# Products of the two first mixers' inputs: pairs of tiles as 2x2 block products with seven multiplications

## The reference, cut to what matters

```python
def even_mixer(x, w_in, w_out):
    h = x @ w_in                                      # 512x1024 times 1024x3584
    rq, rk, rv, rg, sq, sk, sv = jnp.split(h, EVEN_SPLITS, axis=-1)
    ...                                               # rotary on rq, rk; silu on rg; attention
def odd_mixer(x, w_in, w_out, ...):
    h = x @ w_in                                      # 512x1024 times 1024x3072
    q, k, v = jnp.split(h, 3, axis=-1)
```

## Time and profile before

| | us |
|---|---|
| median of 3 runs (lowest, highest) | 2689.16 (2664.75, 2702.93) |
| profiled execution, first to last instruction (its whole time isn't given) | 2679.4 |
| TensorE busy | 2603.0 |
| VectorE, ScalarE, GpSimd busy | 1483.2, 1241.3, 114.9 |
| even_in, first to last matmul | 13.59 to 175.95 |
| odd_in, full tiles | 730.97 to 839.78 |

### The profile page before, as it was taken

The page is one execution under the profiler, slowest core; times in us unless marked ns, Lnnn a source line. Parts: engine busy times, 40 slices in busy tenths (PEclk is TensorE's granted clock), DMA queues, the critical chain, the costliest instruction groups (busy, mean ns, idle before and its releaser), DMA issues.

```text
span 2679.4 us, 51068 instructions
## 1 busy us (share of the span) xinstructions
PE 2603.0 (97%) x20904; PEld 2408.2 (90%) x20904; DVE 1483.2 (55%) x2490; ACT 1241.3 (46%) x2037; POOL 114.9 (4%) x178
## 2 busy tenths in 40 slices
PE   8999999999999999999999999989999999999998
PEld 8985999999997599999989877779966998999998
DVE  5235666543424776664467989862476354544433
ACT  4237344432425844442364887852475243444422
POOL 0000000000000000000001223300000000000000
PEclk9999999999998999999999999999999999999999
DMA  6420122223321023233344665632211231323232
GB/s 198 122 71 1 64 95 94 94 96 106 113 95 63 9 72 102 96 99 118 101 159 147 212 196 186 189 126 97 93 55 56 95 126 41 102 94 97 99 103 71
DMA packets 76142, 278.34 MB, mean 104 GB/s; under 512 B 9802, under 2 KB 12010, under 8 KB 75488
## 3 DMA queue, kind: packets, MB, share of 16 engines
q1 hardware_dynamic: 62112, 217.42, 24.3%
q0 software_dynamic: 13888, 58.88, 7.6%
HBM read 267.03 MB, written 9.24 MB: 103 GB/s over the span
## 4 chain that ended last, share of the span: by engine, by line
PE 77%; DVE 12%; ACT 6%; DMA 3%; issue 2%; POOL 0%; DVEq 0%; SPq 0%; ACTq 0%
PE acc L348 64%; PE acc L379 3%; DMA w_raw<-in_stream 2%; DVE big L1851 1%; PE ps L379 1%; DVE res_tmp L2150 1%; DVE big L2479 1%; ACT res_tmp L2120 1%; DVE w_lo L329 1%; PE acc L1351 1%; DVE big L1503 1%; ACT w_hi L323 1%; DVE res_tmp L2144 1%; PE ps L463 1%; PE ps L769 1%
## 5 line engine op out<-in xcount | busy, mean ns | idle before, releaser
L348 PE MATMUL acc<-x_split,w_hi 128*128 128x256 f32 x7936 | 1242.4, 279 | 7.7 <-ACT big L661 2.9
L348 PEld LDWEIGHTS acc<-x_split,w_hi 128*128 128x128 f32 x7936 | 1061.5, 189 | 10.6 <-issue 7.2
L348 PE MATMUL acc<-x_split,w_lo 128*128 128x256 f32 x3968 | 780.7, 278 | 0.0
L329 DVE TENSOR_TENSOR w_lo<-w_raw,w_hi 128x1024 fp32r<-128x1024 f32 x405 | 494.5, 1222 | 482.1 <-ACT w_hi L323 482.1
L323 ACT ACTIVATE w_hi<-w_raw 128x1024 fp32r<-128x1024 f32 x405 | 427.0, 1055 | 588.5 <-PE acc L348 525.7
L348 PEld LDWEIGHTS acc<-x_split,w_lo 128*128 128x128 f32 x3968 | 602.1, 189 | 0.0
L348 PE MATMUL acc<-big_r,w_hi 128*128 128x256 f32 x3376 | 528.4, 279 | 0.6 <-DVE big_r L2532 0.6
L348 PEld LDWEIGHTS acc<-big_r,w_hi 128*128 128x128 f32 x3376 | 451.7, 189 | 1.5 <-DVE big_r L2532 0.8
L348 PE MATMUL acc<-big_r,w_lo 128*128 128x256 f32 x1688 | 332.8, 279 | 0.0
L348 PEld LDWEIGHTS acc<-big_r,w_lo 128*128 128x128 f32 x1688 | 256.2, 188 | 0.0
L1066 ACT ACTIVATE res_tmp<-acc,par 128x512 f32<-128x512 f32 x84 | 64.8, 772 | 142.5 <-PE acc L348 138.0
(11 more groups left out here) (356 smaller groups left out, 2739.9 us busy)
## 6 DMA issues: line engine op xcount, KB each, us to landing
w_raw<-in_stream SPq DMA_DIRECT2D x405, 512.0 KB, 3.5
res_tmp<-scratch_rows POOLq DMA_DIRECT2D x96, 320.0 KB, 5.2
big<-scratch_rows POOLq DMA_DIRECT2D x32, 320.0 KB, 6.1
scratch_bias<-res_tmp POOLq DMA_DIRECT2D x1, 2560.0 KB, 56.0
res_tmp<-in_x SPq DMA_DIRECT2D x2, 1024.0 KB, 6.8
res_tmp<-scratch_bias POOLq DMA_DIRECT2D x8, 256.0 KB, 4.0
scratch_x<-res_tmp POOLq DMA_DIRECT2D x1, 2048.0 KB, 7.8
scratch_kv<-big POOLq DMA_DIRECT2D x1, 2048.0 KB, 8.3
```

What stands on the lines that cost most here:

```text
L329: dve.tensor_tensor(w_lo[:, u.slot], w_raw[:, u.slot], w_hi[:, u.slot].bitcast(F32), ALU.subtract).then_inc(lo_done, 1)
L348: mm = pe.matmul(a[:, h], w, AR[:, x + k, h], start=(k == 0 and w is wh and x == hi and h.start == 0), stop=(k == total - 1 and w is wl), ...
```

## The change

From tile 9 on (tiles 8 to 27 of even_in, 8 to 23 of odd_in, counted from 0) two tiles are computed as a pair, by Strassen's scheme in its form with few additions. Weights and inputs of a pair are 2x2 blocks: two output tiles by two halves of the 1024 inputs, and two halves of the inputs by two halves of the tokens. Seven block products (form f = 0 to 6) of 4 input blocks, 3 splits and 256 tokens, 12 matmuls each, are accumulated in three half banks a, b and c.

- `strassen_pool`: GpSimd makes four weight sums a pair (f = 1 to 4), each 128x512, in `w_sum`, which lies in the place of `w_lo`. Sum 2 is made from sum 1, sum 3 from sum 2; sum 1 needs both units of the pair.
- `st_hi` (ScalarE) rounds a form, `st_lo` (VectorE) writes its remainder over the sum; remainders 1 and 2 wait until sum 2 and sum 3 have read the sum in that place. The rings are now taken as eight half places: form n goes into place n mod 8, free once the product 8 forms before is done. A raw unit is given back with both of a pair, behind remainder 6.
- `strassen_act`: ScalarE copies three partial sums out of PSUM (snapshots 0 to 2, after products 0 to 2) and the last output quarter; each copy stands behind the rounding of the same form of the next pair. `strassen_dve`: VectorE adds the other three output quarters (additions 0 to 2, after products 3 to 5) between the remainders of the next pair. Product f = 2 to 4 waits for snapshot f - 2, product 6 for additions 0 and 1.
- `t_step`, `t_hi`, `t_lo`: in the first 8 tiles four sums of input blocks are made and split (eight sums and four remainders of 1024 columns on VectorE, four roundings on ScalarE).
- Thirteen semaphores get shared names (`SHARED`), to make room. The stages' matmuls on TensorE are written out instead of looped.

The diff, cut to its core:

```diff
+ST_FIRST, ST_PAIRS = 8, {"even_in": 10, "odd_in": 8}
+        ST_IN = ((XH, XL, 0, 0), (0, None), (1, None), (XH, XL, 4, 1), (2, None), (XH, XL, 4, 0), (3, None))
...
+        def st_place_free(eng, stage, n):
+            if n < 8:
+                tile_done(eng, Units(UB[stage] + ST_FIRST - RING + n // 2))
+            else:
+                st_multiplied(eng, stage, n - 8)
...
+        def strassen_pe(pe, stage):
+            for p in range(ST_PAIRS[stage]):
+                g, u, t = ST_BASE[stage] + p, st_unit(stage, p), st_tile(stage, p)
+                a, b, c = st_banks(t)
+                pe.wait_ge(acc_free[t.bank], t.in_bank + 1)
+                for f, to in enumerate((a, b, a, b, a, c, a)):
+                    if f == 6:
+                        pe.wait_ge(lo_done, u.count + 2)
+                        pe.wait_ge(ev("st_add"), 3 * g + 2)
+                    else:
+                        pe.wait_ge(ev("st_lo"), 6 * g + f + 1)
+                    if 2 <= f <= 4:
+                        pe.wait_ge(ev("st_snap"), 3 * g + f - 1)
+                    if p and f in (1, 5):
+                        pe.wait_ge(ev("st_add"), 3 * g - (2 if f == 1 else 0))
+                    if p == 0 and len(ST_IN[f]) == 2:
+                        pe.wait_ge(ev("t_lo"), 4 * (stage == "odd_in") + ST_IN[f][0] + 1)
+                    wh, wl = st_form(w_hi, 7 * p + f), st_form(w_lo, 7 * p + f)
+                    for k in range(4):
+                        cols = slice(k * P, k * P + P)
+                        for n, (w, lo) in enumerate(((wh, 0), (wh, 1), (wl, 0))):
+                            mm = pe.matmul(to, w[:, cols], st_x(stage, f, lo, k), start=(f in (0, 1, 5) and k == n == 0),
+                                           stop=(k == 3 and n == 2 and f in (3, 5, 6)), skip_group_check=True)
+                    if f == 6:
+                        mm.then_inc(units_used, 2)
+                    else:
+                        mm.then_inc(ev("st_used"), 1)
+        def st_hi(act, stage, p, f):
+            n, g = 7 * p + f, ST_BASE[stage] + p
+            st_place_free(act, stage, n)
+            if f in (0, 5, 6):
+                st_landed(act, stage, p, f // 6)
+                x = st_raw(stage, p, f // 6, f // 5)
+            else:
+                act.wait_ge(ev("st_sum"), 4 * g + f)
+                x = st_form(w_sum, n)
+            ins = act.activation(st_form(w_hi, n), x, ACT.Copy)
+            if f == 6:
+                ins.then_inc(hi_done, 2)
+            else:
+                ins.then_inc(ev("st_hi"), 1)
+        def st_sum(pool, stage, p, f):
+            n, g = 7 * p + f, ST_BASE[stage] + p
+            st_place_free(pool, stage, n)
+            if f == 1:
+                st_landed(pool, stage, p, 0)
+                st_landed(pool, stage, p, 1)
+                x, y, op = st_raw(stage, p, 1, 0), st_raw(stage, p, 1, 1), ALU.add
+            elif f == 2:
+                pool.wait_ge(ev("st_sum"), 4 * g + 1)
+                x, y, op = st_form(w_sum, n - 1), st_raw(stage, p, 0, 0), ALU.subtract
+            elif f == 3:
+                pool.wait_ge(ev("st_sum"), 4 * g + 2)
+                x, y, op = st_raw(stage, p, 0, 1), st_form(w_sum, n - 1), ALU.subtract
+            else:
+                x, y, op = st_raw(stage, p, 0, 0), st_raw(stage, p, 1, 0), ALU.subtract
+            pool.tensor_tensor(st_form(w_sum, n), x, y, op).then_inc(ev("st_sum"), 1)
+        def st_lo(dve, stage, p, f):
+            n, g = 7 * p + f, ST_BASE[stage] + p
+            if f == 6:
+                dve.wait_ge(hi_done, st_unit(stage, p).count + 2)
+                dve.wait_ge(ev("st_sum"), 4 * g + 4)
+            else:
+                dve.wait_ge(ev("st_hi"), 6 * g + f + 1)
+            if f in (1, 2):
+                dve.wait_ge(ev("st_sum"), 4 * g + f + 1)
+            x = st_raw(stage, p, f // 6, f // 5) if f in (0, 5, 6) else st_form(w_sum, n)
+            ins = dve.tensor_tensor(st_form(w_lo, n), x, st_form(w_hi, n).bitcast(F32), ALU.subtract)
+            if f == 6:
+                ins.then_inc(lo_done, 2)
+            else:
+                ins.then_inc(ev("st_lo"), 1)
+        def strassen_act(act, stage, out, scale=None, finish=None):
+            pairs = ST_PAIRS[stage]
+            for p in range(pairs):
+                g, u, t = ST_BASE[stage] + p, st_unit(stage, p), st_tile(stage, p)
+                a, b, c = st_banks(t)
+                by = scale(p) if scale else 1.0
+                after = 0
+                for f in range(7):
+                    if p + 1 < pairs:
+                        st_hi(act, stage, p + 1, f)
+                    if f < 3:
+                        act.wait_ge(ev("st_used"), 6 * g + f + 1)
+                        if f == 0 and p >= 2:
+                            act.wait_ge(ev("st_add"), 3 * (g - 2) + 3)
+                        act.activation(st_snap(stage, p, f), (a, b, a)[f], ACT.Copy, scale=by).then_inc(ev("st_snap"), 1)
+                    if f == 6:
+                        tile_done(act, u, 2)
+                        act.activation(out(p, 1, 0), a, ACT.Silu if finish and p in (2, 3) else ACT.Copy,
+                                       scale=by).then_inc(acc_free[t.bank], 1)
+                    while p + 1 == pairs and after < RING and st_last_form(stage, after) <= 7 * p + f:
+                        st_multiplied(act, stage, st_last_form(stage, after))
+                        split_hi(act, st_unit(stage, pairs) + after)
+                        after += 1
+                if finish:
+                    finish(p)
+        def strassen_dve(dve, stage, out, scale=None):
+            pairs = ST_PAIRS[stage]
+            for p in range(pairs):
+                g, t = ST_BASE[stage] + p, st_tile(stage, p)
+                a, b, c = st_banks(t)
+                by = scale(p) if scale else 1.0
+                after = 0
+                def add(n):
+                    dve.wait_ge(ev("st_used"), 6 * g + 4 + n)
+                    dve.wait_ge(ev("st_snap"), 3 * g + 3 - (n == 1))
+                    to, x = out(p, n == 1, n < 2), (b, a, c)[n]
+                    snap = st_snap(stage, p, (2, 1, 0)[n])
+                    if by == 1.0:
+                        ins = dve.tensor_tensor(to, x, snap, ALU.add)
+                    else:
+                        ins = dve.scalar_tensor_tensor(to, x, by, snap, ALU.mult, ALU.add)
+                    ins.then_inc(ev("st_add"), 1)
+                if p + 1 < pairs:
+                    q = p + 1
+                    st_lo(dve, stage, q, 0)
+                    st_lo(dve, stage, q, 1)
+                    st_lo(dve, stage, q, 2)
+                    add(0)
+                    st_lo(dve, stage, q, 3)
+                    add(1)
+                    st_lo(dve, stage, q, 4)
+                    st_lo(dve, stage, q, 5)
+                    add(2)
+                    st_lo(dve, stage, q, 6)
+                else:
+                    for n in range(3):
+                        add(n)
+                        split_lo(dve, st_unit(stage, pairs) + n)
+                    split_lo(dve, st_unit(stage, pairs) + 3)
+        def strassen_pool(pool, stage):
+            for p in range(ST_PAIRS[stage]):
+                for f in (1, 2, 3, 4):
+                    st_sum(pool, stage, p, f)
...
-                    split_hi(act, u + RING)
+                    if i == 0:
+                        split_hi(act, u + RING)
+                        continue
+                    for f in (2 * j, 2 * j + 1)[:2 - j // 3]:
+                        st_hi(act, "even_in", 0, f)
+                    t_hi(act, "even_in", j)
...
-                split_lo(dve, u + RING)
+                if n < 4:
+                    split_lo(dve, u + RING)
+                    for m in (2 * n, 2 * n + 1):
+                        t_step(dve, "even_in", m)
+                if n == 4:
+                    st_lo(dve, "even_in", 0, 0)
+                if n == 5:
+                    t_lo(dve, "even_in", 0)
+                    st_lo(dve, "even_in", 0, 1)
+                if n == 6:
+                    t_lo(dve, "even_in", 1)
+                    st_lo(dve, "even_in", 0, 2)
+                    st_lo(dve, "even_in", 0, 3)
+                if n == 7:
+                    t_lo(dve, "even_in", 2)
+                    for f in (4, 5, 6):
+                        st_lo(dve, "even_in", 0, f)
+                    t_lo(dve, "even_in", 3)
...
             pool.dma_start(SCR_BIAS, row).then_inc(ev("bias_out"), 16)
+            strassen_pool(pool, "even_in")
             pool.wait_ge(ev("bias_out"), 16)
...
                 pool.dma_start(A[:, DBIAS + h], row).then_inc(ev("bias_in"), 16)
+            strassen_pool(pool, "odd_in")
             pool.wait_ge(ev("g_lo"), 2 * KF)
```

More of the change, by code:

```diff
@@ L58 @@
 HEAD = {"up0": 0, "odd_in": 1, "up1": 2}
+ST_FIRST, ST_PAIRS = 8, {"even_in": 10, "odd_in": 8}
+ST_BASE = {"even_in": 0, "odd_in": 10}
 UB, TB = {}, {}
@@ new lines, in build, with st_unit, st_tile, st_form @@
```

(43 more changed lines are left out.)

162 lines of the change are left out of this document (121 added, 41 removed).

## The result

The median went from 2689.49 us (8 runs, 2662.74 to 2702.93) to **2708.52 us** (8 runs, 2686.69 to 2719.75); the ratio is 1.0077, with an interval of 1.0048 to 1.0107. The forecast was 2702 in a range of 2673 to 2724.

What follows compares the result with a forecast made beforehand. TensorE was taken to bound the kernel (busy 2603.0 of 2679.4 us), with late weight loads in even_in. Even_in +16, odd_in -3.9 and the seam +1 gave +13 on the median: 2702 us, range 2673 to 2724.

Steps and rivals of the forecast that it cites:

- (a): Matmuls in even_in and odd_in: 84 instead of 96 a pair, 9.52 us instead of 10.88, 24.5 us less in all.
- (b): Work beside each pair: sums and remainders wait for each other, last product 1.0 us late, pair 10.5; odd_in -3.9 us.
- the 11 that the forecast had named as a sign of being wrong: Changed profile: pairs 9.5 us apart or over 11 would show the prediction wrong; odd_in pairs about 10.5 apart, right.
- The two rows in which VectorE lost GpSimd's whole length: Later stage, VectorE additions beside GpSimd's: 1.55 us became 3.00, 1.28 became 2.38; a sum's hold was taken as 1.2.
- the row from 1738.40: Later stage: VectorE started 0.27 us before GpSimd yet lost the whole length, cited against the first issuer going first.
- (c): Preparing inputs in the first 8 tiles: in even_in VectorE at 5.5 us against 5.44, a lag under a microsecond.
- (d): Loads in even_in: units 12 and 13 asked for at 67 to 68, landing late; stage ends at 191.9, 16 us later.
- the gap: Weights' queue in even_in: after a gap the next load pays 22.9 us again; rival, nothing anew: 2692 us, chance 0.20.
- the table load: In even_in, 1.28 us ahead of a snapshot, with two gate activations: 1 us towards the stage's end.
- (e): End of even_in: two splits instead of one after the last product, 1 us on the path to the next stage.
- without a hold-up: Rival: sums and remainders don't hold each other up, pairs 9.5 us apart; 2687 us, chance 0.15.
- holds of 1.86: Rival: each sum holds for all of 1.86 us, the last product of a pair 3.4 late; 2738 us, chance 0.10.

Runs made afterwards that it cites:

- the additions beside the kernel before: Kernel before, plus 32 unused GpSimd additions from SBUF at the start of odd_in: remainders 1.27 to 2.39 us meanwhile, odd_in 125.6 us in both.
- the small write: Relative-position bias write of 16 rows a head instead of 128: changed kernel 2679.60 us, ratio 1.0021; kernel before 2682.12 us, ratio 1.0009.
- the mixture: Changed kernel: 16-row bias write, 64 loads; even_in additions 0, 1 before remainder 2; odd_in sums on VectorE; first pairs' snapshots before roundings: 2653.04 us, ratio 0.9907.

## Why the prediction was right, point by point

*(a)* Right. An undisturbed product takes 1.36 us, 0.1133 a matmul.

*(b)* Right in the mechanism, too low in size. The last product waits for the pile on VectorE, which comes of sums and remainders that exclude one another. At the first collision the order was not the one forecast (remainder 1 went ahead of sum 3), which changes nothing, since both are ready at the same moment and the pile is as long either way; at the second it was (sum 4 ahead of remainder 2), in all steady pairs. A pair took 11.03 where 10.5 was forecast, just over the 11 that the forecast had named as a sign of being wrong. The half microsecond is made of small terms: the sums took 1.29 to 1.38 undisturbed (1.2 taken), so that addition 1 was done 9.43 us into the pair (9.2 forecast); the last product started 0.14 behind it and took 1.46 to the next one's start (1.36). The delays of the products in between don't count, since the last one waits for VectorE and not for them. The first pair of odd_in took 12.2. So odd_in's own length changed by +0.9 instead of -3.9; 1.2 of these 4.8 us is made up again by the time the next stage is under way, which leaves -0.3. The two rows in which VectorE lost GpSimd's whole length had the cause in them, and the additions beside the kernel before show it again without any of the new products.

The rule of the Trainium skill (SBUF — State Buffer, "Who interferes with whom") that a VectorE instruction with two SBUF operands contends with a GpSimd instruction that reads SBUF, and not with one that only writes it, agrees with both halves of the experiment: 1.70 us beside sums, 0.69 at most beside constants. On the order of grants, whoever has the earlier record goes first in the pair shown: remainder 1 (808.79) ahead of sum 3 (808.83), sum 4 (810.60) ahead of remainder 2 (810.74). That agrees with the other rule of the Trainium skill from that section, which the prediction cites and which stands there at VectorE's two-port modes: whoever issues first gets the shared pair. Why the row from 1738.40 went the other way stays open.

*(c)* Too low, and covered. "A lag under a microsecond" was wrong for the first pair: TensorE stood four times in pair 0 of the changed kernel (1.28, 1.64, 0.29 and 3.77 us between two matmuls). As far as the rows show it cost nothing there, since unit 13, behind the bias write (which ended at 94.7), held TensorE until 98 in any case; with the small write and the sums on VectorE the same work shows as 4.5 and 3.6 us, and takes nearly all that the products give in even_in.

*(d)* Right. Unit 12 was asked for at 69.3 (67 to 68 forecast), took 23.3 us, so the gap did cost anew; product 3 of pair 1 started at 98.13 (98.2), and the stage ended at 192.88 (191.9). That the end is so close is in part luck, since errors offset one another. Behind 98.13 the clock cost 2.0 us in two products, not 3.1, and the last product of pair 1 wasn't late; the seven pairs from 105.4 on were longer, 11.1 us together above 9.52 each. That is 13.1 where 12.1 was forecast (3.1 for the clock, 1 for the table load, 8 for late products). With the small write the unit is asked for as late (69.9) and no such stand is left, so the transfer made it.

*(e)* Not seen, and small. The next stage's first matmul (176.22 before) comes 16.9 us later, as much as the end of even_in; the microsecond forecast at that seam isn't there. 0.5 us arises later, in stages that the change leaves alone: odd_in starts 17.4 us later.

Sum: by the traces +18.3 us at the last matmul of odd_in and +17.2 in the next stage, +19.0 by the medians, +13 forecast. By the traces the difference, some 4 us, is odd_in (3.6) and the end of even_in (1.0), less 0.5 for (e); the rest of the medians' difference is within their noise. The rivals: without a hold-up the pairs would have been 9.5; holds of 1.86 did occur (1.81 for sum 3), but that length contains the wait for a remainder, as the forecast's argument had it.

## What to carry to other kernels

When work goes to an idle engine, ask what it shares with the busy one: look for rows in which the two already work at once, and price the new work by what the other lost there, not by its own length. A hold-up costs only what waits behind it, so put what TensorE waits for next ahead of what it wants later before moving work elsewhere. And a saving in a stage that is about to run short of loads is eaten there; look at what gives buffers back before counting it.

## What the runs showed of the hardware that was not expected

Stretches of the same matmuls run at one of two paces, at a granted clock of 1.00 in both cases, and which one changes from execution to execution without any change in their code. The chain in the same later stage, of the kernel before and then of the changed one:

```profile
1012.95 87.10 PE acc L348 x766
```
```profile
1019.48 100.58 PE acc L367 x854
```

That is 0.1137 and 0.1178 us a matmul. A stage of 3102 matmuls took 366 us in most of the profiled executions and 353 in three of them (the changed kernel with the small write, the kernel before with the GpSimd additions, the mixture). The two profiled spans differ by 38.4 us where the medians differ by 19.0: behind odd_in the changed kernel's execution ran two more stages at the slower pace, which are 17.6 of the 21.2 us that come on there. The paces may also be what spreads the runs of one kernel, but only one execution of each has a trace, so that isn't shown. What sets the pace stays open.
